# Nine of eleven quads of an up-projection by Strassen's scheme, in a decoder layer on one Trainium2 core

## The reference

```python
def swiglu(h, w1, w3, w2):
    return (jax.nn.silu(h @ w1) * (h @ w3)) @ w2

h = modulate(rms_norm(x, g_ffn2[i]), sh3, sc3)
x = x + 0.5 * (1.0 + gt3[:, None, :]) * swiglu(h, w1_ffn2[i], w3_ffn2[i], w2_ffn2[i])
return rms_norm(x, g_final)
```

## Time and profile before

| what | value |
|---|---|
| median of three runs | 1129.64 us |
| span of the profiled execution, first to last instruction | 1128.4 us |
| busy: TensorE, VectorE, ScalarE, GpSimd | 99%, 50%, 45%, 16% of the span |
| second FFN's up-projection | about 757 to 1003 us |
| down-projection and end | about 1003 to 1128 us |

### The profile page before, as it was taken

The page is one execution under the profiler, slowest core; times in us unless marked ns, Lnnn a source line. Parts: engine busy times, 40 slices in busy tenths (PEclk is TensorE's granted clock), DMA queues, the critical chain, the costliest instruction groups (busy, mean ns, idle before and its releaser), DMA issues.

```text
span 1128.4 us, 14854 instructions
## 1 busy us (share of the span) xinstructions
PE 1114.7 (99%) x5462; PEld 906.7 (80%) x5462; DVE 565.0 (50%) x916; ACT 509.1 (45%) x886; POOL 184.0 (16%) x115
## 2 busy tenths in 40 slices
PE   7999999999999999999999999999999999999998
PEld 5678888888888888877778888888888888888887
DVE  4544454545344475579986636677333333332232
ACT  4565646465445434246557755444323223222233
POOL 0055454545444511000000000040000000000000
PEclk9999999999999999999999999999999999999999
DMA  9845655565555224222222123222422332333222
GB/s 325 274 153 198 220 173 170 195 220 187 177 177 177 74 75 141 56 57 75 57 57 63 50 75 94 75 75 79 144 75 74 118 105 74 112 116 103 79 75 76
DMA packets 159692, 138.27 MB, mean 123 GB/s; under 512 B 3623, under 2 KB 157858, under 8 KB 159650
## 3 DMA queue, kind: packets, MB, share of 16 engines
q1 hardware_dynamic: 131376, 109.33, 30.8%
q10 hardware_dynamic: 28274, 28.38, 7.6%
HBM read 135.59 MB, written 2.10 MB: 122 GB/s over the span
## 4 chain that ended last, share of the span: by engine, by line
PE 94%; DVE 2%; ACT 2%; issue 0%; ACTq 0%; DVEq 0%
PE ps L388 28%; PE ps L390 28%; PE ps L389 28%; PE ps L1321 2%; PE ps L1299 1%; PE ps L1286 1%; PE ps L1266 1%; PE ps L1093 1%; DVE w_lo L367 1%; DVE nrm L445 1%; ACT w_hi L362 1%; PE ps L523 1%; ACT ada L763 1%; PE ps L673 0%; PE ps L675 0%; PE ps L674 0%
## 5 line engine op out<-in xcount | busy, mean ns | idle before, releaser
L367 DVE TENSOR_TENSOR w_lo<-raw,w_hi 128x1024 fp32r<-128x1024 f32 (+1 forms) x164 | 239.3, 1459 | 382.6 <-ACT w_hi L362 382.4
L388 PE MATMUL ps<-h_hi,w_hi 128*128 128x512 f32 x1008 | 398.7, 396 | 2.3 <-DVE h_lo L451 2.0
L390 PE MATMUL ps<-h_hi,w_lo 128*128 128x512 f32 x1008 | 393.2, 390 | 0.0
L389 PE MATMUL ps<-h_lo,w_hi 128*128 128x512 f32 x1008 | 392.8, 390 | 0.0
L362 ACT ACTIVATE w_hi<-raw 128x1024 fp32r<-128x1024 f32 (+1 forms) x164 | 183.6, 1120 | 353.9 <-PE ps L390 353.9
L388 PEld LDWEIGHTS ps<-h_hi,w_hi 128*128 128x128 f32 x1008 | 189.3, 188 | 49.4 <-issue 7.2
L390 PEld LDWEIGHTS ps<-h_hi,w_lo 128*128 128x128 f32 x1008 | 189.2, 188 | 40.1
L389 PEld LDWEIGHTS ps<-h_lo,w_hi 128*128 128x128 f32 x1008 | 189.5, 188 | 37.3 <-issue 0.2
L388 PE MATMUL ps<-g_hi,w_hi 128*128 128x512 f32 x330 | 129.8, 393 | 0.2 <-issue 0.2
L390 PE MATMUL ps<-g_hi,w_lo 128*128 128x512 f32 x330 | 128.7, 390 | 0.0
L389 PE MATMUL ps<-g_lo,w_hi 128*128 128x512 f32 x330 | 128.5, 390 | 0.0
(11 more groups left out here) (241 smaller groups left out, 1035.9 us busy)
## 6 DMA issues: line engine op xcount, KB each, us to landing
raw<-in_w_ffn SPq DMA_DIRECT2D x42, 1024.0 KB, 5.2
ada<-in_w_ada ACTq DMA_DIRECT2D x27, 1024.0 KB, 5.0
raw<-in_w_ffn SPq DMA_DIRECT2D x16, 1408.0 KB, 6.2
raw<-in_w_in SPq DMA_DIRECT2D x64, 256.0 KB, 3.2
ada<-in_w_ada SPq DMA_DIRECT2D x16, 512.0 KB, 8.9
raw<-in_w_out SPq DMA_DIRECT2D x16, 256.0 KB, 3.0
x_tok<-in_x SPq DMA_DIRECT2D x4, 512.0 KB, 5.5
raw<-in_w_ffn SPq DMA_DIRECT2D x8, 256.0 KB, 7.6
```

Of the source, the lines that this page charges most:

```text
L367: nc.vector.tensor_tensor(tiles_of(w_lo[j % SPL], nk), raw_of(f, j, nk), tiles_of(w_hi[j % SPL], nk).bitcast(F32), ALU.subtract).then_inc( ...
L388: nc.tensor.matmul(ps[:, bank, :], hi, rhs_hi, start=start, stop=False)
L389: nc.tensor.matmul(ps[:, bank, :], hi, rhs_lo, start=False, stop=False)
L390: return nc.tensor.matmul(ps[:, bank, :], lo, rhs_hi, start=False, stop=stop)
```

## The change

The first two quads stay. Of the other nine quads, the two column tiles of one matrix form a **set**: a 1024 x 256 block of weights times the 512 tokens. It is seen as 2 x 2 blocks: weights a, b (the first and second four k-tiles of the first column tile), c, d (the same of the second), tokens in two halves of 256. Strassen's scheme (in the form with seven products and shared sums) gives the four corners of the output from seven products instead of eight: a, s1, s4, s2, d, b, s3 in the order of `pe_set`. One product is 4 k-tiles times three passes, 12 matmuls of 256 columns. A set has 84 of them where it had 48 of 512 columns.

- The weight sums s1 = c + d, s3 = a - c, s2 = s1 - a, s4 = b - s2 are made by GpSimd (`pool_sums`), four 128x512 operations a set, into `raw_sum` and over c. Each of the seven weight blocks has one buffer for its high and one for its low half (`blk_hi`, `blk_lo`); the next set's half waits for this set's product.
- The token sums t1 to t4 are made once, by seven 128x1024 operations of GpSimd (`pool_tokens`), and split by ScalarE and VectorE (`token_hi`, `token_lo`). The first four normalised tiles are now kept in `u_a`.
- The products are put together on VectorE and ScalarE: ScalarE copies the product a (x1), VectorE adds (`dve_middle`, `dve_lower`, `dve_upper`). The product s4 is computed in the next set (`late_product`), after that set's a and s1, once `dve_lower` has read the bank. The last one stands inside the first unit of the down-projection. silu, g, g_hi and g_lo are done for two tiles at a time.
- The block buffers lie over w_hi, w_lo and xT. So SyncE writes x (2 MB) to DRAM ahead of the sets and reads it back near their end.

```diff
-U_DOWN = [44, 152]
+U_DOWN = [44, 116]
+SETS = 18
+QUADS = SETS // 2
+BL = KD // 2
+HS = SEQ // 2
...
+        def scaled_tile(n, k):
+            return u_a[:, k, :] if n == 2 and k < BL else nrm[:, k % 4, :]
...
+        PLACE = {"a": 0, "s1": 1, "s2": 3, "d": 4, "b": 5, "s3": 6, "s4": 9}
+        LAST_PRODUCT = 7 * SETS
+        BANKS = ((0, 4, 5, 1), (2, 6, 7, 3))
...
+        def raw_block(name, m):
+            w = raw2_view(m, KD)
+            return {"a": w[:, 0:BL, 0:P], "b": w[:, BL:KD, 0:P], "c": w[:, 0:BL, P:2 * P], "d": w[:, BL:KD, P:2 * P],
+                    "s1": raw_sum[m][:, :, :], "s2": raw_sum[m][:, :, :], "s3": w[:, 0:BL, P:2 * P], "s4": raw_sum[m][:, :, :]}[name]
...
+        def block_hi(act, name, q, m):
+            n = number(name, q, m)
+            if name == "a":
+                act.wait_ge(raw2_in[m], 16 * (q + (U_UP[1] // 4 + 2 - ROUNDS_MIX)))
+            if name in SUMS:
+                act.wait_ge(bsum_done, 8 * q + (4 * m + SUMS[name]))
...
+            nc.scalar.activation(tiles_of_block(blk_hi[name]), raw_block(name, m), ACT.Copy).then_inc(bhi_done, 1)
+        def block_lo(dve, name, q, m):
+            dve.wait_ge(bhi_done, number(name, q, m))
+            nc.vector.tensor_tensor(tiles_of_block(blk_lo[name]), raw_block(name, m), tiles_of_block(blk_hi[name]).bitcast(F32),
+                                    ALU.subtract).then_inc(blo_done, 1)
...
+        def pool_sums(pool, q, m):
+            pool.wait_ge(raw2_in[m], 16 * (q + (U_UP[1] // 4 + 2 - ROUNDS_MIX)))
+            if not (isinstance(q, int) and q == 0):
+                pool.wait_ge(blo_done, number("s4", q - 1, m))
+            x = raw_sum[m][:, :, :]
+            nc.gpsimd.tensor_tensor(x, raw_block("c", m), raw_block("d", m), ALU.add).then_inc(bsum_done, 1)
+            pool.wait_ge(bsum_done, 8 * q + (4 * m + 1))
+            nc.gpsimd.tensor_tensor(raw_block("c", m), raw_block("a", m), raw_block("c", m), ALU.subtract).then_inc(bsum_done, 1)
+            pool.wait_ge(blo_done, number("s1", q, m))
+            nc.gpsimd.tensor_tensor(x, x, raw_block("a", m), ALU.subtract).then_inc(bsum_done, 1)
+            pool.wait_ge(blo_done, number("s2", q, m))
+            nc.gpsimd.tensor_tensor(x, raw_block("b", m), x, ALU.subtract).then_inc(bsum_done, 1)
...
+        def pool_tokens(pool):
+            a1, a2 = u_a[:, :, 0:HS], u_a[:, :, HS:SEQ]
+            b1, b2 = nrm[:, :, 0:HS], nrm[:, :, HS:SEQ]
+            shift_a, shift_b = [mods[:, 48 + BL * i:48 + BL * (i + 1)].unsqueeze(2).broadcast_to([P, BL, HS]) for i in range(2)]
+            t1, t2, t3, t4 = [t[:, :, :] for t in t_raw]
+            pool.wait_ge(unit_done, done(U_UP[1] + 1))
+            pool.wait_ge(u_done, 2 * KD + BL)
+            nc.gpsimd.tensor_tensor(t1, a2, a1, ALU.subtract).then_inc(t_step, 1)
+            pool.wait_ge(u_done, 3 * KD)
+            nc.gpsimd.tensor_tensor(t4, b1, b2, ALU.subtract).then_inc(t_step, 1)
+            pool.wait_ge(hlo_done, 3 * KD)
+            nc.gpsimd.tensor_tensor(b2, b2, shift_b, ALU.add).then_inc(t_step, 1)
+            pool.wait_ge(t_step, 3)
+            nc.gpsimd.tensor_tensor(t2, b2, t1, ALU.subtract).then_inc(t_step, 1)
+            nc.gpsimd.tensor_tensor(a2, a2, shift_a, ALU.add).then_inc(t_step, 1)
+            pool.wait_ge(t_step, 5)
+            nc.gpsimd.tensor_tensor(t3, b2, a2, ALU.subtract).then_inc(t_step, 1)
+            nc.gpsimd.tensor_tensor(t4, t4, t1, ALU.add).then_inc(t_step, 1)
...
+        def tokens_of(name):
+            if name == "a":
+                return h_hi[:, 0:BL, 0:HS], h_lo[:, 0:BL, 0:HS]
+            if name == "b":
+                return h_hi[:, BL:KD, 0:HS], h_lo[:, BL:KD, 0:HS]
+            if name == "s4":
+                return h_hi[:, BL:KD, HS:SEQ], h_lo[:, BL:KD, HS:SEQ]
+            if name == "d":
+                return h_hi[:, T4_AT[0], T4_AT[1]], h_lo[:, T4_AT[0], T4_AT[1]]
+            return {"s1": (t1_hi, t1_lo), "s2": (t2_hi, t2_lo), "s3": (t3_hi, t3_lo)}[name]
...
+            for kk in range(BL):
+                hi, lo = [w[name][:, kk * P:(kk + 1) * P] for w in (blk_hi, blk_lo)]
+                nc.tensor.matmul(dst, hi, t_hi[:, kk, :], start=fresh and kk == 0, stop=False, skip_group_check=not fresh)
+                nc.tensor.matmul(dst, hi, t_lo[:, kk, :], start=False, stop=False, skip_group_check=not fresh)
+                last = nc.tensor.matmul(dst, lo, t_hi[:, kk, :], start=False, stop=kk == BL - 1, skip_group_check=not fresh)
...
+        def late_product(pe, q, m):
+            pe.wait_ge(comb_done, 8 * q + (4 * m + 3))
+            product(pe, "s4", q, m, BANKS[m][2], False)
+        def pe_set(pe, q, m):
+            c11, p4, p5, u1 = BANKS[m]
+            if isinstance(q, int) and q == 0:
+                pe.wait_ge(g_done, KF + 5 + m)
+            else:
+                pe.wait_ge(pre_done, 4 * q + (2 * m - 2))
+                pe.wait_ge(comb_done, 8 * q + (4 * m - 4))
+            product(pe, "a", q, m, c11, True)
+            if first_set(q, m):
+                pe.wait_ge(tlo_done, 1)
+            product(pe, "s1", q, m, p5, True)
+            if not first_set(q, m):
+                late_product(pe, *before(q, m))
+            if first_set(q, m):
+                pe.wait_ge(tlo_done, 2)
+            product(pe, "s2", q, m, u1, True)
+            if first_set(q, m):
+                pe.wait_ge(tlo_done, 4)
+            product(pe, "d", q, m, p4, True)
+            pe.wait_ge(pre_done, 4 * q + (2 * m + 1))
+            product(pe, "b", q, m, c11, False)
+            pe.wait_ge(comb_done, 8 * q + (4 * m + 1))
+            product(pe, "s3", q, m, u1, False)
...
+            nc.vector.tensor_tensor(u1_sb[:, :], ps[:, BANKS[m][3], 0:HS], x1_sb[:, :], ALU.add).then_inc(comb_done, 1)
...
+            nc.vector.tensor_tensor(x1_sb[:, :], ps[:, u1, 0:HS], x1_sb[:, :], ALU.add).then_inc(comb_done, 1)
+            dve.wait_ge(comb_done, 8 * q + (4 * m + 2))
+            nc.vector.tensor_tensor(tmp[:, 1 + 2 * m, :].rearrange("p (h n) -> p h n", h=2), ps[:, p4:p5 + 1, 0:HS],
+                                    x1_sb[:, :].unsqueeze(1).broadcast_to([P, 2, HS]), ALU.add).then_inc(comb_done, 1)
...
+        def dve_upper(dve, q, m):
+            dve.wait_ge(prod_done, number("s4", q, m))
+            nc.vector.tensor_tensor(tmp[:, 2 * m, HS:SEQ], ps[:, BANKS[m][2], 0:HS], u1_sb[:, :], ALU.add).then_inc(comb_done, 1)
...
+        def act_set(act, q, m):
+            nq, nm = after(q, m)
+            if not first_set(q, m):
+                block_hi(act, "s3", q, m)
+                act_first_product(act, q, m)
+            if not last_set(q, m):
+                block_hi(act, "a", nq, nm)
+                block_hi(act, "s1", nq, nm)
+            block_hi(act, "s4", q, m)
+            if not last_set(q, m):
+                block_hi(act, "s2", nq, nm)
+            if m == 1:
+                act_silu(act, q)
+            if not last_set(q, m):
+                block_hi(act, "d", nq, nm)
+                block_hi(act, "b", nq, nm)
+            act_corner(act, q, m)
+            if m == 0 and not first_set(q, m):
+                act_ghi(act, q - 1)
...
+            sets(act, act_set)
+            act.wait_ge(prod_done, number("d", QUADS - 1, 1))
+            hi_u(act, U_DOWN[1])
+            act_ghi(act, QUADS - 1)
+            act.wait_ge(prod_done, LAST_PRODUCT)
+            act.wait_ge(comb_done, 4 * SETS)
+            hi_u(act, U_DOWN[1] + 1)
...
+                sp.wait_ge(x_done, 3 * KD)
+                sp.dma_start(x_spill, xT[:, :, :]).then_inc(x_kept, 16)
+                sp_sets(sp)
...
+                sp.wait_ge(blo_done, number("s3", q - 1, m))
+                sp.wait_ge(bsum_done, 4 * (2 * (q - 1) + m) + 4)
+            sp.dma_start(raw2_view(m, KD), w_up[1][m][:, :, bass.ds(2 * P * q + 4 * P, 2 * P)]).then_inc(raw2_in[m], 16)
...
+                    if f == 1 and isinstance(i, int) and i + j == 0:
+                        unit(0, 0, g_hi, g_lo, nk=4, stop=False)
+                        late_product(pe, QUADS - 1, 1)
+                        for kk in range(4, KH):
+                            last = mm3(0, 0, kk, g_hi[:, kk, :], g_lo[:, kk, :], False, False)
+                        last.then_inc(unit_done, 1)
```

309 lines of the change are left out of this document (286 added, 23 removed).

## The result

| | before | after |
|---|---|---|
| median | 1129.49 us (four runs, 1129.20 to 1129.79) | 1150.85 us (four runs, 1150.22 to 1151.57) |
| ratio, 95% interval | | 1.0189 (1.0175 to 1.0203) |
| span of the profiled execution | 1128.4 us | 1149.0 us |

The change makes the kernel **21.4 us slower**; forecast was 1133.9, with a range up to 1142. The direction was right and the time was not.

What follows compares the result with a forecast made beforehand. The prediction took TensorE, busy 99%, to bound the old kernel. Loop -2.5 (matmul saving less VectorE's lost turns), second FFN's start +3.7 and joint +3.1 sum to +4.3 on 1129.6: 1133.9 us, range 1122 to 1142.

Steps and rivals of the forecast that it cites:

- turns with GpSimd: In the loop, VectorE's two-input instructions alternate with GpSimd's sums, about 1.1 us a turn; VectorE loses 7.1 us a quad.
- Matmuls: Nine looped quads on TensorE: 20.16 instead of 21.76 us each, 14.5 us saved if nothing on TensorE waits.
- rival 3: Product boundaries in the loop cost TensorE 0.11 us each, 13.9 us for 126, giving 1135.8 us; chance 0.08.
- VectorE's own work: Low halves, g products and PSUM combinations in the loop: 14.3 us a quad on VectorE, which alone fits.
- The middle quads: Seven quads in the middle of the loop, set by VectorE's cycle: 21.8 us each.
- The first and last quad: Both ends of the loop have fewer sums to share with: taken at 20.4 us each.
- The start: Start of the second FFN: token sums delay VectorE's h_lo and w_lo, +3.7 us, bounds 0 to 7.2.
- The part for h_lo: Second FFN's start: two token sums delay the last h_lo low halves, +1.6 us each.
- The joint: Change to the down-projection: 2.05 us waiting for its first weights, then 1.0 us longer; +3.1 us, 2 to 5.
- Rival 2: Turns in the loop cost more: 22.4 us a quad gives 1142.2 us, no sum hidden 1147; chance 0.12.
- Rival 1: Sums are covered by VectorE's waits and PSUM steps, TensorE never late in the loop: 1121.9 to 1126.8 us; chance 0.33.

Runs made afterwards that it cites:

- e1: Changed kernel with GpSimd's weight sums of the eight looped quads cut to one element a row, semaphores kept: 1134.3 us.
- e4: Changed kernel with all four weight sums of each set made by VectorE instead of GpSimd, token sums left on GpSimd: 1130.4 us.
- e10: Changed kernel with GpSimd's looped weight sums cut to one element a row, four small GpSimd instructions ahead of each as a delay: 1133.5 us.
- e9: Changed kernel with the two chained weight sums per set (s2, s4) moved to VectorE, the other two left on GpSimd: 1136.6 us.
- e8: Changed kernel with weight and token sums on VectorE, reordered at the second FFN's start (1124.4 us), then also three moves at the joint: 1121.5 us.
- e3: Changed kernel with GpSimd's seven token sums at the second FFN's start cut to one element a row: 1144.6 us.
- e7: Changed kernel with GpSimd's looped weight sums cut to one element a row, nine small GpSimd instructions ahead of each as a delay: 1159.2 us.

## Why the prediction was wrong

The sum was -14.5 for the matmuls and what waiting gives back, and it missed by 16.3 us of span (20.6 against 4.3). The mechanism, turns with GpSimd that make TensorE wait for `dve_lower`, was right; three terms were too small, and one cost, TensorE's clock after its waits, was in none of them. Term by term:

- **Matmuls, right.** A quad without waits is 20.16 us in e1, e4 and e10; spacing and saving are as taken from the earlier trace rows. The same 20.16 us refutes rival 3: they leave nothing for borders.
- **VectorE's own work, nearly right.** In the undisturbed quad of 857.2 to 879.5 us it is 14.5 us by spacing, for a forecast 14.3.
- **The middle quads, mis-sized.** The step is "VectorE's cycle is 14.3 + 7.1 + 0.45 = 21.8". VectorE's cycle is 22.34 us. The turns came in the forecast places and with the forecast size (6.5 us, and 0.55 of waiting for d's high half, for 7.1). Own work is 0.2 longer, and the waits for the high half of a take 0.7 instead of 0.45: 0.5 us a quad too short, 3.6 in seven. The rest is the clock: the walk took a wait of TensorE at its length alone, but in two of the seven quads its clock fell after it, 0.9 us each. 158.4 against 7 x 21.8 = 152.6: 5.8 us.
- **The first and last quad, mis-sized.** "I take 20.4 each" was no calculation. They took 204.3 - 158.4 = 45.9 us, 5.1 more: the first has TensorE waiting 3.15 us at 825.0 and 0.8 at 814.1, and a clock of 0.92 over 22 us. That VectorE enters the loop late there, with the token tiles' low halves still to make, fits but was not varied by itself. The wait of 3.15 stays in e1, whose first quad keeps its full sums, and is 2.1 in e4 and 0.75 in e9.
- **The start, mis-sized.** 9.0 us for a forecast 3.7, outside even its bounds of 0 to 7.2. The part for h_lo was about right: 3.2 forecast, and TensorE waits 1.15 and 1.68 us for two h_lo and 0.17 for the w_lo behind the first. The step that failed is "a w_lo of the next units may come 0 to 2 us late, I take 0.5": five sums follow each other almost without a pause (777.9 to 790.9), and each two-input instruction of VectorE beside them loses its turn, two w_lo and the product with the shift. TensorE waits 1.78 and 1.58 us for two w_lo, and after the first of them its clock is at 0.51 for 3.4 us, which costs 1.7.
- **The joint, right**: 3.2 for 3.1, with TensorE's two waits at 1.96 and 1.01 for a forecast 2.05 and 1.0; e8 took 3.0 of it back.

The clock's share over all three places is an estimate of mine: 1.7 us at the start (3.4 us at half speed), 1.7 in the first quad, 1.8 in the two long ones, so about 5 of the 16.3.

Rival 2 named 22.4 us a quad and 1142 us. The quad is the measured one but for the clock, by luck: its reason is not, since a turn costs 1.1 us and not the whole records. Its start and ends were as short as mine. Rival 1 is refuted by 15.0 us of waits in front of the late s4 product. Its condition, VectorE's sums under the rest, becomes true in e4, by taking GpSimd out.

What stays open: what decides whether the clock falls. It fell after waits of 1.93 us at 903 and 971, and not after one of 1.93 at 881 or of 1.95 at 949. After the first wait at the joint (1.96 us) it stayed at 1.00 after the change and fell in e3 and e9 (0.51 from 1001.0 to 1004.4 us in e9). So the length of the wait alone does not decide it, and no run varied anything else. And e10's delays are 0.2 us short of the real ones, so that a small share of the delay alone isn't excluded.

## What to carry to other kernels

Work given to an idle GpSimd isn't free when VectorE's instructions read two SBUF operands: count up to one whole turn of VectorE per GpSimd instruction (1.1 us for 128x512 here, 6.5 for eight), and ask whether VectorE would do it faster itself (0.61). A delay through a second engine that costs nothing while its neighbours have slack (e10) need not stay free when turns use that slack up. At places where an engine enters or leaves a loop, walk the order through as for the middle: the guessed start and the guessed first and last quad were 5.3 and 5.1 us short, almost as much each as the seven middle quads together.

## What was not expected of the hardware

- GpSimd's smallest instructions take turns too: a 128x4 sum takes 0.20 to 0.21 us free and 0.66 behind a 0.69 us low half, so nine in a row took 2.75 us on average in e7.
- After waits of 1.93 and 3.15 us TensorE's granted clock was at 0.50 for 3.4 us, with 0.21 us between matmuls of 256 columns instead of 0.12, but not after each such wait. Two waits of the same length, each with a stretch behind it:

```profile
880.81 0.38 PE L676 MATMUL ps<-h_hi,s_hi 128*128 128x256 f32 x1 [1.93 <-DVE tmp L765]
...
903.15 0.38 PE L676 MATMUL ps<-h_hi,s_hi 128*128 128x256 f32 x1 [1.93 <-DVE tmp L765]
```

```profile
881.40:884.80 3.40, 3.40 (x31) 3.40 (x30) 3.15 (x5) 1.74 (x4) 1.30 (x1) 1.00 0.56 157
903.70:907.10 3.40, 3.40 (x18) 3.40 (x17) 2.48 (x4) 1.40 (x3) 1.29 (x1) 0.50 0.62 164
```

  The Trainium skill (TensorE: Matmul & The Clock Gate, The HAM clock gate) says that the clock drops when TensorE has been idle; the rows agree in that each of the drops read here followed a wait of TensorE, and not every such wait brought one. Where it did, the wait cost up to 1.7 us more than its own length at the start, and 0.9 in a middle quad.
